# Compression products on column halves with gelu after the turn, eviction shared by two engines, and some low halves on GpSimd

## The reference, cut to what matters

```python
def nsa_compress(kv, pos, w1, w2):          # kv: 512 tokens, 2 heads, 64
    halves = kv.reshape(b, t // 16, 16, hk, d)
    win = jnp.concatenate([halves[:, :-1], halves[:, 1:]], axis=2) + pos[:, None, :]
    flat = jnp.moveaxis(win, 3, 2).reshape(b, 31, hk, 32 * d)
    return jax.nn.gelu(flat @ w1) @ w2      # (31, 2048) @ (2048, 256) @ (256, 64), keys and values
```

## Time and profile before

| | |
|---|---|
| time, median of 3 runs | 2407.98 us (2405.62 to 2409.56) |
| the profiled execution's own time | 2406.93 us |
| its span, first to last instruction | 2405.1 us |
| TensorE busy | 2292.6 us, 95% |
| VectorE busy | 1208.7 us, 50% |
| ScalarE busy | 901.8 us, 37% |
| GpSimd busy | 82.5 us, 3% |
| mean granted TensorE clock | 0.982 of full speed |

### The profile page before, as it was taken

How to read it: one execution, slowest core, us unless ns; L and a number is a source line. 1 busy time by engine, 2 the same in 40 slices (tenths; PEclk the granted TensorE clock), 3 DMA queues, 4 the chain that set the end, 5 groups by cost and what they waited for, 6 DMA issues and landing times. The chain is left out here.

```text
span 2405.1 us, 27598 instructions
## 1 busy us (share of the span) xinstructions
PE 2292.6 (95%) x10816; PEld 1806.7 (75%) x10816; DVE 1208.7 (50%) x1990; ACT 901.8 (37%) x1483; POOL 82.5 (3%) x119
## 2 busy tenths in 40 slices
PE   7999999899989999998989999998989899999988
PEld 5888887776656888887768888877766568888876
DVE  5444433466676444433554443345566764444335
ACT  5222223444654323222452322244455542222233
POOL 0000000032000000000000000001310000000000
PEclk9999999999999999999999999999999999999999
DMA  4433334212102333333223333343120023333322
GB/s 154 146 96 97 90 98 152 87 60 65 42 27 72 96 103 91 93 99 105 79 78 97 96 95 97 98 132 100 53 77 27 25 81 98 97 97 98 98 94 70
DMA packets 68986, 214.31 MB, mean 89 GB/s; under 512 B 8143, under 2 KB 15311, under 8 KB 68858
## 3 DMA queue, kind: packets, MB, share of 16 engines
q1 hardware_dynamic: 59344, 189.27, 26.1%
q10 hardware_dynamic: 9514, 23.27, 2.9%
HBM read 208.30 MB, written 5.40 MB: 89 GB/s over the span
## 5 line engine op out<-in xcount | busy, mean ns | idle before, releaser
L501 PE MATMUL main<-xh,wh 128*128 128x512 f32 x1944 | 781.5, 402 | 20.9 <-DVE xl L1407 19.7
L502 PE MATMUL main<-xl,wh 128*128 128x512 f32 x1944 | 763.2, 393 | 0.0
L503 PE MATMUL main<-xh,wl 128*128 128x512 f32 x1944 | 763.0, 392 | 0.0
L1400 DVE TENSOR_TENSOR wl<-raw,wh 128x1024 fp32r<-128x1024 f32 (+3 forms) x372 | 440.2, 1184 | 402.7 <-ACT wh L948 402.2
L948 ACT ACTIVATE wh<-raw 128x1024 fp32r<-128x1024 f32 (+3 forms) x372 | 378.1, 1017 | 499.6 <-PE main L503 465.4
L501 PEld LDWEIGHTS main<-xh,wh 128*128 128x128 f32 x1944 | 368.9, 190 | 128.0 <-issue 25.8
L502 PEld LDWEIGHTS main<-xl,wh 128*128 128x128 f32 x1944 | 369.1, 190 | 78.9 <-issue 5.5
L503 PEld LDWEIGHTS main<-xh,wl 128*128 128x128 f32 x1944 | 368.7, 190 | 78.6
L501 PE MATMUL main<-ffh,wh 128*128 128x512 f32 x704 | 273.9, 389 | 0.0
L502 PE MATMUL main<-ffl,wh 128*128 128x512 f32 x704 | 273.9, 389 | 0.0
L503 PE MATMUL main<-ffh,wl 128*128 128x512 f32 x704 | 273.9, 389 | 0.0
(11 more groups left out here) (230 smaller groups left out, 1937.8 us busy)
## 6 DMA issues: line engine op xcount, KB each, us to landing
raw<-in_ffn_gate SPq DMA_DIRECT2D x88, 512.0 KB, 3.6
raw<-in_ffn_up SPq DMA_DIRECT2D x88, 512.0 KB, 3.6
raw<-in_ffn_down SPq DMA_DIRECT2D x64, 448.0 KB, 3.3
raw<-in_w_in_t SPq DMA_DIRECT2D x40, 512.0 KB, 3.6
raw<-in_ffn_down SPq DMA_DIRECT2D x32, 512.0 KB, 3.5
raw<-in_wout SPq DMA_DIRECT2D x24, 384.0 KB, 3.1
w<-in_cmp_w ACTq DMA_DIRECT2D x16, 512.0 KB, 3.7
raw<-in_ple_gate SPq DMA_DIRECT2D x16, 512.0 KB, 3.2
```

The costliest lines, as they stand in the source:

```text
L501: nc.tensor.matmul(out, lh, rh, start=start, stop=False, **kw)
L502: nc.tensor.matmul(out, lh, rl, start=False, stop=False, **kw)
L503: return nc.tensor.matmul(out, ll, rh, start=False, stop=stop, **kw)
L1400: nc.vector.tensor_tensor(wl[:, c % SLOTS, 0:n], raw[:, c % SLOTS, 0:n], wh[:, c % SLOTS, 0:n], ALU.subtract).then_inc(*tick("weights_lo", ...
```

## The change

- `w2c` and `hidT` get 32 places a head instead of 31; GpSimd clears `w2c` once a layer. Pair m of a part now goes to rows 0 to 63 of the bank where m is even, and to rows 64 to 127 where it is odd, in two sums side by side.
- ScalarE copies the 128x256 bank to `hid` (`cmp_halves`). TensorE's turn is now a product with `fold`, two identities one under the other, which turns and adds the halves. Gelu is applied behind it, from the turned bank straight into `hidT`; VectorE's copy is gone. Gelu for keys is in ScalarE's step 5, ahead of the third forget gate; for values at the start of step 10.
- Two of the four `natC` banks are emptied by VectorE, two by ScalarE.
- The low halves of group B's five tiles and of twelve `wout` chunks (17 a layer) are computed by GpSimd, after its HGRN work. The places of these splits in VectorE's list are skipped.

```diff
+ON_GPSIMD = {(tile,) for tile in GROUP_OF["B"]} | {key for key in CHUNKS if key[0].startswith("wout")}
+def low_half(c):
+    return "weights_lo_pool" if EVERY[c][1] in ON_GPSIMD else "weights_lo"
...
-                        sp.wait_ge(*done("weights_lo", c - SLOTS, layer="all"))
+                        sp.wait_ge(*done(low_half(c - SLOTS), c - SLOTS, layer="all"))
...
+                    nc.gpsimd.memset(w2c[:], 0.0).then_inc(*tick("zeros", "w2c"))
...
+                    for c, (own, key) in enumerate(EVERY):
+                        if own == layer and key in ON_GPSIMD:
+                            n = chunk_width(key)
+                            pool.wait_ge(*done("weights_hi", c, layer="all"))
+                            nc.gpsimd.tensor_tensor(wl[:, c % SLOTS, 0:n], raw[:, c % SLOTS, 0:n],
+                                                    wh[:, c % SLOTS, 0:n], ALU.subtract).then_inc(
+                                                        *tick("weights_lo_pool", c, layer="all"))
...
-                        mm = nc.tensor.matmul(hidden[kv][0:n2, 0:CMP_HIDDEN], w2c[:, m, :],
-                                              w1[:, k % W1_SLOTS, m % 4, :],
-                                              start=(m == 0), stop=(m == PAIRS - 1))
+                        rows = slice(HEAD * (m % 2), HEAD * (m % 2) + HEAD)
+                        mm = nc.tensor.matmul(hidden[kv][rows, 0:CMP_HIDDEN], w2c[:, m, :],
+                                              w1[:, k % W1_SLOTS, m % 4, :], start=(m < 2), stop=False,
+                                              skip_group_check=True)
...
-                        mm = nc.tensor.transpose(out[:, k * n2:(k + 1) * n2], hid[0:n2, k * P:(k + 1) * P],
-                                                 const_("ident")[0:n2, 0:n2])
+                        mm = nc.tensor.matmul(out[:, k * HEAD:(k + 1) * HEAD], hid[:, k * P:(k + 1) * P],
+                                              sm("fold", 0, HEAD), start=True, stop=True)
...
-                        for t in range(QT):
+                        for t in (0, 2):
...
+                def cmp_halves(kv):
+                    act.wait_ge(*done("cmp_part", 4 * kv + 3))
+                    if kv:
+                        act.wait_ge(*done("cmp_turned", 0))
+                    nc.scalar.activation(hid[:], bank_of(("hidden", kv))[:, 0:CMP_HIDDEN],
+                                         ACT.Copy).then_inc(*tick("cmp_halves", kv, frees=("hidden", kv)))
...
                 def cmp_gelu(kv):
-                    act.wait_ge(*done("cmp_part", 4 * kv + 3))
-                    nc.scalar.activation(hid[0:2 * NCMP, :], bank_of(("hidden", kv))[0:2 * NCMP, 0:CMP_HIDDEN],
+                    act.wait_ge(*done("cmp_turned", kv))
+                    if kv:
+                        act.wait_ge(*done("cmp_made", 0))
+                    nc.scalar.activation(hidT[:].rearrange("p k n -> p (k n)"),
+                                         bank_of(("hiddenT", kv))[:, 0:4 * CPAD],
                                          ACT.Gelu_apprx_tanh).then_inc(
-                                             *tick("cmp_gelu", kv, frees=("hidden", kv)))
+                                             *tick("cmp_gelu", kv, frees=("hiddenT", kv)))
...
                     for step in range(STEPS["C"]):
+                        if step == 10:
+                            cmp_gelu(1)
                         project("C", step)
...
                         if step == 4:
+                            cmp_halves(0)
+                        if step == 5:
                             cmp_gelu(0)
...
-                            cmp_gelu(1)
+                            cmp_halves(1)
...
+                            if low_half(c) != "weights_lo":
+                                at["lo"] += 1
+                                continue
...
+                        for t in (1, 3):
+                            key = ("nat" + group, t, "out")
+                            o = bank_of(key)
+                            nc.vector.tensor_scalar(hv[:, t, :, :], o[:, 0:3 * P].rearrange("p (a d) -> p a d", a=3),
+                                                    sm("rt", t), None, ALU.mult).then_inc(
+                                                        *tick("values_v", "C", t, 0))
+                            nc.vector.tensor_scalar(gates[:, t, :], o[:, 384:402], sm("rt", t), None,
+                                                    ALU.mult).then_inc(*tick("values_v", "C", t, 3, frees=key))
...
-                        if step == 5:
-                            cmp_hidden(0)
```

More of the change, by code:

```diff
@@ L300, in layers @@
         c2 = sb("c2", [P, 2, 2, SEQ])
-        w2c = sb("w2c", [P, PAIRS, 2 * NCMP])
+        w2c = sb("w2c", [P, PAIRS, 2 * CPAD])
         w1 = sb("w1", [P, W1_SLOTS, 4, CMP_HIDDEN])
@@ L305, in layers @@
         hid = sb("hid", [P, CMP_HIDDEN])
-        hidT = sb("hidT", [P, 2, 2 * NCMP])
+        hidT = sb("hidT", [P, 2, 2 * CPAD])
         assert place["at"] <= ckv_at
@@ L506, in chunk @@
                     c, n = counts.layer * NCHUNKS + CHUNK[key], chunk_width(key)
-                    pe.wait_ge(*done("weights_lo", c, layer="all"))
+                    pe.wait_ge(*done(low_half(c), c, layer="all"))
                     return wh[:, c % SLOTS, 0:n], wl[:, c % SLOTS, 0:n]
@@ L687, in hgrn @@
                             turn_compressed()
-                n2 = 2 * NCMP
                 hidden = {}
@@ L706, in cmp_turn @@
                     out = take(("hiddenT", kv))
[L707 removed]
+                    pe.wait_ge(*done("cmp_halves", kv))
+                    pe.wait_ge(*done("fold", layer=0))
                     for k in range(2):
[L709 to L710 removed]
+                        mm = nc.tensor.matmul(out[:, k * HEAD:(k + 1) * HEAD], hid[:, k * P:(k + 1) * P],
+                                              sm("fold", 0, HEAD), start=True, stop=True)
                     mm.then_inc(*tick("cmp_turned", kv))
@@ L721, in cmp_make @@
                             pad = w2p[:, kv, k, 1 - g:3 - g, :].rearrange("p a d -> p (a d)")
-                            part = hidT[:, k, g * NCMP:(g + 1) * NCMP]
+                            part = hidT[:, k, g * CPAD:g * CPAD + NCMP]
                             if kv == 0:
@@ L1064, in project @@
                         log_tables()
-                        act.wait_ge(*done("values", "C", QT - 1, 3))
+                        act.wait_ge(*done("values", "C", 2, 3))
+                        act.wait_ge(*done("values_v", "C", 3, 3))
                         nc.scalar.activation(gates[:], gates[:], ACT.Exp,
@@ L1433, in small_exponents @@
                 def small_exponents():
+                    V = nc.vector
+                    if counts.layer == 0:
+                        dve.wait_ge(const_in, 16)
+                        ident = const_("ident")
+                        V.tensor_tensor(sm("fold", 0, HEAD), ident[:, 0:HEAD], ident[:, HEAD:P],
+                                        ALU.add).then_inc(*tick("fold"))
                     dve.wait_ge(params_in[counts.layer], 32)
-                    V = nc.vector
                     V.tensor_scalar(sm("gq"), col("nq"), HEAD ** -0.5, None, ALU.mult).then_inc(*tick("gains", 0))
@@ L1568, in project @@
                         split(CHUNK[("nat" + group, step - len(names))] + AHEAD)
+                    if step == len(names) + 3:
+                        dve.wait_ge(*done("product", ("nat" + group, 3)))
+                        dve.wait_ge(*done("factor_turned"))
+                        for t in (1, 3):
[6 more added lines that the diff above has]
+                                                    ALU.mult).then_inc(*tick("values_v", "C", t, 3, frees=key))
                     if 0 < step <= len(names) and names[step - 1] in NORMED:
```

18 lines of the change are left out of this document (4 added, 14 removed).

## The result

The changed kernel takes **2377.97 us** (median of 4 runs, 2374.20 to 2382.71), the kernel before on the same chip 2408.77 (2405.62 to 2411.61). The ratio is 0.987, 95% interval 0.986 to 0.989. The forecast was 2380, range 2368 to 2394.

A forecast was written before the change was run, and what follows sets the result against it. TensorE, busy 95% of the span, was taken as the bound. Per layer, group C -7.8, low halves -6.8 and GpSimd's cost +0.5 gave -14.1, -28 us in all, so 2380 us, range 2368 to 2394.

The forecast's parts named there:

- Stall gone, chain 3.3 us earlier, new wait: Group C: 4.33 us stall before `cmp_make(0)` goes, about 6 us wait before `kc`'s head sums comes; step 8 6.8 us earlier.
- Part 7: Group C, compression's last part, behind the new wait: side-by-side column halves save 0.9 us a layer.
- slow clock: Group C: the idle wait brings back TensorE's lower clock, costing 0 to 2.3 us a layer, taken as 1.2.
- eviction: End of group C: emptying `natC` banks on two engines saves 1.3 us a layer before `natA`'s first product.
- HGRN's end: At 571.01 a VectorE low half of 1.22 us moves away, cutting TensorE's 2.59 us wait by 1.1 a layer.
- Attention: Waits behind VectorE's low halves in units 0, 1, 2 and 4 shrink by 2.8, 1.2, 0.8 and 0.9 us a layer.
- GpSimd holding VectorE: VectorE operations with two SBUF inputs are held to a GpSimd low half's end; +0.5 us a layer, bounds 0 and +6.
- GpSimd's low halves, 2.9 and 2.1 us: Length of a GpSimd low half, scaled by columns from a 128x256 row: 2.9 us for 128x1024, 2.1 for 128x768.
- relief in attention is eaten: Rival: VectorE is held by GpSimd or TensorE meets ScalarE; only group C and 571.01 gain; 2390 us, chance 0.2.
- halves don't run side by side: Rival: the column halves write one bank and don't overlap, so group C gains only 4 us a layer; 2387 us, chance 0.06.
- better than forecast: Rival: shorter chain in group C, clock kept high, output projection gains 2 us; 2372 us, chance 0.14.
- slower: Rival: GpSimd's low halves hold VectorE's scaling in attention, up to 25.5 us a layer; 2430 us, chance 0.1 with nothing gained.

The follow-up runs named there:

- Run 3: Changed kernel with the compression's sixteen products a part ordered eight into the lower column half, then eight into the upper, instead of alternating; 2384.59 us.
- run 4: Changed kernel with the first gelu put back behind the third forget gate in ScalarE's list; 2383.69 us.
- run 12: Changed kernel with GpSimd's low halves of units 1 to 4 waiting for VectorE's first scaling; the wait was always over, so same order; 2371.93 us.
- run 1: Changed kernel with all low halves back on VectorE, the rest of the change kept; 2391.75 us.
- run 7: Changed kernel with GpSimd computing each low half twice into the same place; 2377.62 us.
- run 9: Changed kernel unaltered, measured again on the chip of run 12; 2376.20 us.
- run 6: Changed kernel with `kc` copied earlier, gate's second half later, `natC` high half between gate halves, weight loads in step 5, `hq2` scaled before the low half; 2362.93 us.
- run 11: Changed kernel with only the output projection's twelve chunks split on GpSimd, group B's five tiles back on VectorE; 2390.40 us.

## Why the prediction was right

The time, 2377.97, is 2 us below the forecast. That the number is so near is in part luck: the two places gave 32.1 us where the sum had 29.2 ahead of GpSimd's +0.5 a layer, and some 4 us were lost again elsewhere. The steps came out as follows, per layer.

- **Stall gone, chain 3.3 us earlier, new wait: -6.8.** Right, and in its parts. The third gate at 430.9 foretold, 431.25 found; square's end at 443.1 and 443.41; a wait of 6 us and 5.48; step 8 at 445.9 and 446.06. Step 8 is 6.6 us earlier than before. What it started on was the end of part 6, slow at the low clock (444.14, 1.98 us); the bank of `hq2`, which the prediction took for the limit, was scaled by 445.81, 0.25 us ahead. Run 3 shows that the halves are needed for it, run 4 that the move is.
- **Part 7, -0.9; slow clock, +1.2; eviction, -1.3.** The first products of step 8 ran at the low clock, which cost 0.9: part 7 starts at 451.51 instead of 457.25, only 5.7 earlier. Part 7 itself gave 0.9 (1.08 instead of 1.94). Eviction gave 1.23 (1.86 to 0.63; the sign named was 0.5 or less). C in all: -7.9 against -7.8.
- **HGRN's end, -1.1.** Measured -1.1 (the wait went from 2.59 to 1.45).
- **Attention, -2.8 - 1.2 - 0.8 - 0.9 = -5.7.** Measured -6.8. From HGRN's end to unit 2's start 4.5 against 4.0, unit 2 0.8 against 0.8; unit 4 1.05 against 0.9; and 0.44 at unit 3, where the kernel before waits 0.36 us and I had counted nothing. In H: -7.9 against -6.8. In layer 1 H is 9.0 shorter, by another path: there a wait of 1.24 us near HGRN's end (578.12 in layer 0) is gone too, though not by the change alone, since run 12 has it with the same order (H of layer 1: 191.35); and the slow stretch behind unit 1's wait, which I counted in both layers, was not there before the change (clock 1.00 from 1801 to 1810).
- **GpSimd holding VectorE, +0.5.** Two operations a layer were held in the changed kernel, neither on TensorE's path: VectorE idles again 0.2 and 0.8 us after the second, and TensorE's next wait is 2.16 us where run 1, without such low halves, has 2.08. GpSimd's low half and the operation that begins inside it, twice:

```profile
716.18 1.81 POOL L490 TENSOR_TENSOR wl<-raw,wh 128x768 fp32r<-128x768 f32 x1 [1.47 <-ACT wh L963]
717.13 0.88 DVE L1870 TENSOR_SCALAR small<-small 128x4 f32<-128x4 f32 x1
```

```profile
745.64 2.31 POOL L490 TENSOR_TENSOR wl<-raw,wh 128x768 fp32r<-128x768 f32 x1 [3.04 <-ACT wh L963]
746.16 2.34 DVE L1453 TENSOR_TENSOR acc<-sq 128x512 f32<-128x512 f32 x1
```

  L1870 takes 0.23 us elsewhere and L1453 0.69; both end at or 0.5 us after GpSimd's end. For unit 0 the prediction worked out a hold of 0.6 us, from a low half of 2.9 us. It did not come: the low half ended at 599.62, and the first operation that it could have held, the 128x8 product, started at 599.81. With 2.9 us it would have ended at 600.15. So this place was missed by 0.2 us and thanks to a length that the prediction had too long; that is luck, and run 7 shows what lies on the other side: 3.1 us in H.
- **GpSimd's low halves, 2.9 and 2.1 us.** Too long. Free of VectorE they take 2.36 and 1.81; the means with what VectorE holds them are 2.44 and 1.93. By these two lengths an operation costs about 2.15 ns a column and 0.16 us besides, an estimate that gives 0.71 us for 128x256. The row I scaled from has 0.72, so the error was to multiply the fixed part by four. The estimate that I set aside, 2.2 us from the Trainium skill's "GPSIMD Engine Reference" (Elementwise — side-by-side cycle accounting), was the nearer one. TensorE never waited for a low half of GpSimd in H; what the shorter length was worth is said in the point above.

H and C together are -15.8 in layer 0 and -16.3 in layer 1, where the sum had -14.6 before the +0.5. The profiled execution lost 28.0 us, not 32.1: in layer 0 the shift grew to 15.8 us at unit 4 and fell to 12.3 by the second feed-forward block and 11.5 by layer 1's first; in layer 1 it grew to 27.8 and nearly held (27.4 by the second feed-forward block, 28.0 at the end). In layer 0's units 6 and 7 of the changed kernel the clock was low for some 10 us:

```profile
673.00:683.00 10.00, 9.23 (x36) 6.13 (x38) 7.91 (x25) 4.79 (x9) 2.16 (x1) 0.51 0.13 42
```

The same work in the kernel before, some 16 us later, had 0.83:

```profile
689.00:699.00 10.00, 8.96 (x52) 5.68 (x52) 8.41 (x25) 5.42 (x13) 0.00 (x0) 0.83 0.12 40
```

Run 1 has that longer low stretch without any low half on GpSimd (0.52 from 685 to 695), and runs 9 and 12 differ in such stretches with the same order. So it is not a price of either half of the change; what decides how long such a stretch lasts stays open.

Of the **rivals**, "relief in attention is eaten" (2390) falls by H; "halves don't run side by side" by run 3; "better than forecast" (2372) fails in its mechanism, since the output projection gained next to nothing (in run 12 the shift against the kernel before is 15.2 us at unit 5 and 15.3 in the second feed-forward block), but its number is within what the clock scatters: run 12 took 2371.93 with the order of the changed kernel; "slower" stayed away, in unit 0 by 0.2 us, and run 7 has its mechanism. One thing I did not look for: the 6 us wait was taken as given, and a few moves take another 7 us a layer (run 6).

## What to carry to other kernels

When a stall is removed, follow the chain to the next late operand, and then ask what in each in-order list merely stands ahead of that operand: a copy of 0.2 us that is ready 11 us before its turn (`kc`, made at 431.3, copied at 442.91) is a wait that costs nothing to remove. Time spent on an engine that idles for another is free: here gelu with two table loads, 2.84 us, cost the chain 0.4. And compare distances between fixed points of the trace, since end times of one and the same order differ by 4 us on one chip here.

## What the runs showed of the hardware

- Products of 64 weight columns that alternate between the two column halves ran side by side in one bank: eight of 256 columns in 1.08 us with the tail, 1.94 when all eight went into one half. They did not have to be neighbours: in run 3 four products of the upper half ran beside the last four of the lower that stood ahead of them in the list.
- A VectorE operation begun while GpSimd computed was held to GpSimd's end if it read two tensors from SBUF (128x8: 2.34 us instead of 0.17) or was a `tensor_scalar` (128x4: 0.88 instead of 0.23). By the Trainium skill ("SBUF — State Buffer", Who interferes with whom) both kinds share GpSimd's ports; the rows agree, also in that operations with an input from PSUM were not held: 62 such begun beside low halves of the changed kernel, none over 1.03 times its usual length. Nor was a reciprocal of 128x8 in SBUF (0.19 us at 716.91, as elsewhere). No row shows a large `tensor_scalar` held. It goes the other way too: the low half begun at 574.61 inside a VectorE product of two SBUF tensors took 3.1 us instead of 2.36.
- A switch of ScalarE's tables cost 1.28 us and no more: the high half ends at 428.35, the load starts at 428.37, gelu at 429.66.
- The same order of work took 2371.93 and 2376.20 us on one chip. In the two profiled executions (2367.7 and 2374.8 us) the clock differed in layer 1's last units (0.97 and 0.90). The same wait of 2.1 us was followed by the low clock in run 1 (0.72) and not in run 11 (1.00).
